# Dilated attention of a two-block transformer: tokens taken by residue modulo 4, 24 key tiles a head in place of 40

## The reference, cut to what matters

```python
ATTN_PATTERNS = ((128, 1), (512, 4), (2048, 16))      # (window, dilation); radius = window // (2 * dilation) = 64
...
# query at position p attends to p + j*dilation for j in [-radius, radius]
for g, (window, dilation) in enumerate(ATTN_PATTERNS):
    o_g, lse_g = dilated_window_attention(q[:, :, sl], k[:, :, sl], v[:, :, sl], dilation, window // (2 * dilation))
...
w_mix = jax.nn.softmax(jnp.stack(lses, axis=0), axis=0)
y_b = jnp.sum(w_mix[..., None] * o_all, axis=0)
```

## Time and profile before

| | |
|---|---|
| time of the runs | median 2284.1 us of three (2280.25 to 2287.16) |
| span of the profiled execution | 2278.1 us |
| what lies around the span | 6.0 us to the median, 2.2 to 9.1 us to the single runs |
| PE busy in the span | 2131.4 us (94%) |
| PEld busy | 1818.3 us (80%) |
| DVE, ACT busy | 963.5 us (42%), 830.5 us (36%) |
| attention stage | from 89.3 us to 430.2 us of the span |

### The profile page before, as it was taken

How to read it: one execution, slowest core, us unless ns; L and a number is a source line. 1 busy time by engine, 2 the same in 40 slices (tenths; PEclk the granted TensorE clock), 3 DMA queues, 4 the chain that set the end, 5 groups by cost and what they waited for, 6 DMA issues and landing times. The chain is left out here.

```text
span 2278.1 us, 27535 instructions
## 1 busy us (share of the span) xinstructions
PE 2131.4 (94%) x11313; PEld 1818.3 (80%) x11313; DVE 963.5 (42%) x1315; ACT 830.5 (36%) x1132; POOL 0.2 (0%) x4
## 2 busy tenths in 40 slices
PE   6899999999799999878888899999999978999999
PEld 5688888788788888777677888888779878888887
DVE  3544543233544434445653434434433334344343
ACT  4222332322432333336564343333344443423332
POOL 0000000000000000000000000000000000000000
PEclk9999999999899999988898999999999989999999
DMA  5222212123133222211011222332222212223222
GB/s 183 66 78 63 65 49 72 56 93 102 57 100 105 97 92 92 67 39 42 20 38 38 74 93 93 106 96 92 78 71 75 75 38 75 92 93 109 92 92 76
DMA packets 168319, 178.51 MB, mean 78 GB/s; under 512 B 5921, under 2 KB 138606, under 8 KB 168114
## 3 DMA queue, kind: packets, MB, share of 16 engines
q1 hardware_dynamic: 168088, 177.36, 24.6%
q10 hardware_dynamic: 154, 0.04, 0.0%
HBM read 175.29 MB, written 2.10 MB: 78 GB/s over the span
## 5 line engine op out<-in xcount | busy, mean ns | idle before, releaser
L83 PE MATMUL psum<-norm_T_hi,weights_hi 128*128 128x512 f32 x1184 | 469.1, 396 | 13.9 <-PEq L435 6.4
L85 PE MATMUL psum<-norm_T_hi,weights_lo 128*128 128x512 f32 x1184 | 462.0, 390 | 0.0
L84 PE MATMUL psum<-norm_T_lo,weights_hi 128*128 128x512 f32 x1184 | 461.8, 390 | 0.0
L83 PE MATMUL psum<-weights_hi,act_T_hi 128*128 128x512 f32 (+2 forms) x976 | 369.1, 378 | 8.4 <-DVE weights_lo L286 4.1
L84 PE MATMUL psum<-weights_lo,act_T_hi 128*128 128x512 f32 (+2 forms) x976 | 367.4, 376 | 0.0
L85 PE MATMUL psum<-weights_hi,act_T_lo 128*128 128x512 f32 (+2 forms) x976 | 367.2, 376 | 0.0
L1014 ACT ACTIVATE weights_hi<-raw_weights 128x2048 fp32r<-128x2048 f32 x96 | 183.5, 1911 | 359.7 <-PE psum L85 359.7
L83 PE MATMUL psum<-weights_hi,norm_T_hi 128*128 128x256 f32 (+2 forms) x928 | 267.9, 289 | 9.1 <-PEq L784 4.1
L83 PEld LDWEIGHTS psum<-norm_T_hi,weights_hi 128*128 128x128 f32 x1184 | 223.0, 188 | 64.8 <-issue 14.5
L1035 DVE TENSOR_TENSOR weights_lo<-raw_weights,weights_hi 128x2048 fp32r<-128x2048 f32 x96 | 220.1, 2293 | 111.3 <-ACT weights_hi L1014 111.1
L84 PE MATMUL psum<-weights_lo,norm_T_hi 128*128 128x256 f32 (+2 forms) x928 | 262.8, 283 | 0.0
(11 more groups left out here) (229 smaller groups left out, 1990.3 us busy)
## 6 DMA issues: line engine op xcount, KB each, us to landing
raw_weights<-in_ffn_w_dram SPq DMA_DIRECT2D x64, 1024.0 KB, 5.2
raw_weights<-in_w_in_dram SPq DMA_DIRECT2D x36, 512.0 KB, 4.5
raw_weights<-in_w_up_dram SPq DMA_DIRECT2D x16, 1024.0 KB, 5.4
raw_weights<-in_w_down_dram SPq DMA_DIRECT2D x16, 1024.0 KB, 5.1
raw_weights<-in_w_in_dram SPq DMA_DIRECT2D x12, 1024.0 KB, 5.1
raw_weights<-in_mlstm_w_in_dram SPq DMA_DIRECT2D x8, 1024.0 KB, 5.2
raw_weights<-in_w_out_dram SPq DMA_DIRECT2D x4, 1024.0 KB, 5.8
raw_weights<-in_mla_w_o_dram SPq DMA_DIRECT2D x4, 1024.0 KB, 5.3
```

Source lines behind the costliest of these rows:

```text
L83: pe.matmul(out, ah, bh, start=start, stop=False)
L84: pe.matmul(out, ah, bl, start=False, stop=False)
L85: return pe.matmul(out, al, bh, start=False, stop=stop)
```

## The change

Every tile of 128 tokens in this stage now holds the tokens of one residue modulo 4 (tokens t, t+4, t+8, ...) and no longer 128 neighbours.

- For groups 1 and 2 (dilation 4 and 16) only the key tile of the query's own residue is needed; group 0 (dilation 1) now needs all four. `key_tiles` gives 4 + 1 + 1 = 6 tiles for each query tile, 24 a head.
- Scores are three matmuls of 512, 128 and 128 columns into bank 2 and the first half of bank 3. The mask step is two operations, not three, and the maximum over the parts is folded into the scaling. `turn` and `values` take 6 tiles; ACT copies one bank and DVE half a bank.
- Fills 0 to 5 still multiply contiguous tokens. ACT writes their result to SBUF with a stride, so that queries and keys lie by residue.
- Fills 6 to 8 take their stationary operand with a stride: `tt` is every fourth token of `NTH` and `NTL`, 16 bytes apart.
- `store` reads PSUM with a stride on ACT and on DVE to put the tokens back in order. Mask and rotary tables are laid out anew; the mask table shrinks from 3 x 896 to 1152 columns.

```diff
 def key_tiles(g, t):
-    r = (RADIUS * DIL[g] + P - 1) // P
-    return max(0, t - r), min(NT, t + r + 1)
+    return (0, NT) if g == 0 else (t, t + 1)
...
                         for q, t in enumerate((2 * (f - 6), 2 * (f - 6) + 1) if f < 8 else range(NT)):
-                            tt = slice(t * P, t * P + P)
+                            tt = slice(t, S, NT)
...
-                        for g in range(NG):
+                        for g, at_bank in enumerate((PS[:, 2, :], PS[:, 3, 0:P], PS[:, 3, P:2 * P])):
                             lo, hi = key_tiles(g, t)
-                            mm = pe.matmul(PS[:, 2 + g, 0:(hi - lo) * P], QK[:, h % 2, g, 0, t * P:t * P + P],
+                            mm = pe.matmul(at_bank, QK[:, h % 2, g, 0, t * P:t * P + P],
...
-                            act.activation(QK[:, h % 2, f // 2, f % 2, :], bank, ACT.Copy).then_inc(ev.sem, 1)
+                            act.activation(QK[:, h % 2, f // 2, f % 2, :].rearrange("p (r i) -> p i r", r=NT),
+                                           bank.rearrange("p (i r) -> p i r", r=NT), ACT.Copy).then_inc(ev.sem, 1)
...
-                        act.activation(AH[:, 4 + h, :], PS[:, 6, :], ACT.Copy).then_inc(th.sem, 1)
+                        act.activation(AH[:, 4 + h, :], PS[:, 6, :].rearrange("p (r i) -> p i r", r=NT), ACT.Copy).then_inc(th.sem, 1)
...
-                            for b in (0, 2):
-                                act.wait_ge(ptr.sem, ptr.at(3 * i + b + 1))
-                                w = min(512, m - 512 * b)
-                                act.activation(PT[:, 512 * b:512 * b + w], PS[:, 2 + b, 0:w], ACT.Copy).then_inc(pte.sem, 1)
+                            act.wait_ge(ptr.sem, ptr.at(2 * i + 1))
+                            act.activation(PT[:, 0:512], PS[:, 2, :], ACT.Copy).then_inc(pte.sem, 1)
...
-                        dve.tensor_tensor(AL[:, 4 + h, :], PS[:, 6, :], AH[:, 4 + h, :].bitcast(F32), SUB).then_inc(tl.sem, 1)
+                        dve.tensor_tensor(AL[:, 4 + h, :], PS[:, 6, :].rearrange("p (r i) -> p i r", r=NT),
+                                          AH[:, 4 + h, :].bitcast(F32).rearrange("p (i r) -> p i r", r=NT), SUB).then_inc(tl.sem, 1)
...
-                            dve.tensor_reduce(mall, mx, AX.X, MAXOP).then_inc(a1.sem, 1)
-                            dve.wait_ge(a1.sem, a1.at(i + 1))
-                            dve.tensor_scalar(nm, mall, -scale, None, MUL).then_inc(smx.sem, 1)
+                            dve.wait_ge(smk.sem, smk.at(2 * (i + 1)))
+                            dve.tensor_scalar(nm, mx[:, 0:1], mx[:, 1:2], -scale, MAXOP, MUL).then_inc(smx.sem, 1)
...
-                            dve.tensor_copy(PT[:, 512:1024], PS[:, 3, :]).then_inc(bcd.sem, 1)
+                            dve.tensor_copy(PT[:, 512:768], PS[:, 3, 0:2 * P]).then_inc(bcd.sem, 1)
```

More of the change, by code:

```diff
@@ L34 @@
 NEG = -1e30
-MW = 896
+MW = 1152
 DIL = (1, 4, 16)
@@ L201, in build @@
         IDENT = sb("ident", [P, P])
-        MASK = sb("masks", [P, NG, MW], BF16)
+        MASK = sb("masks", [P, MW], BF16)
         CM = sb("chunk_masks", [P, 2, S])
@@ L205, in build @@
         SCR = sb("scratch", [P, 16384])
-        MRAW = SCR[:, 10240:10240 + NG * MW]
+        MRAW = SCR[:, 10240:10240 + MW]
         SM = sb("small", [P, 512])
@@ L505, in _ @@
                     dve.wait_ge(c_cast.sem, c_cast.at(32))
-                    dve.tensor_copy(MASK[:, :, :], MRAW.rearrange("p (g w) -> p g w", g=NG)).then_inc(smk.sem, 1)
+                    dve.tensor_copy(MASK[:, :], MRAW).then_inc(smk.sem, 1)
                     dve.wait_ge(rt.sem, rt.at(1))
@@ L544, in dilated @@
             VN = SCR[:, 6144:9216].rearrange("p (b t e) -> p b t e", b=2, t=NT)
-            SB = SCR[:, 9216:10624]
-            PT = SCR[:, 10624:12032]
+            NK = 6
+            SB = SCR[:, 9216:9216 + NK * P]
+            PT = SCR[:, 10624:10624 + NK * P]
             ON = SCR[:, 12032:12544].rearrange("p (t e) -> p t e", t=NT)
@@ L549, in dilated @@
             R1 = SCR[0:32, 13568:14592].rearrange("p (j s) -> p j s", j=2)
-            mx, mall = SM[:, 32:35], SM[:, 36:37]
+            mx = SM[:, 32:34]
             nm = SM[:, 38:39]
@@ L603, in scores @@
                         if i:
-                            pe.wait_ge(pte.sem, pte.at(2 * i))
+                            pe.wait_ge(pte.sem, pte.at(i))
                             pe.wait_ge(bcd.sem, bcd.at(i))
-                        for g in range(NG):
+                        for g, at_bank in enumerate((PS[:, 2, :], PS[:, 3, 0:P], PS[:, 3, P:2 * P])):
                             lo, hi = key_tiles(g, t)
-                            mm = pe.matmul(PS[:, 2 + g, 0:(hi - lo) * P], QK[:, h % 2, g, 0, t * P:t * P + P],
+                            mm = pe.matmul(at_bank, QK[:, h % 2, g, 0, t * P:t * P + P],
                                            QK[:, h % 2, g, 1, lo * P:hi * P], start=True, stop=True)
@@ L624, in values @@
                             pe.wait_ge(ev.sem, ev.at(NFILL * (h + 1)))
-                        pe.wait_ge(pte.sem, pte.at(2 * i + 2))
+                        pe.wait_ge(pte.sem, pte.at(i + 1))
                         pe.wait_ge(bcd.sem, bcd.at(i + 1))
@@ L744, in _ @@
                             dve.wait_ge(sc.sem, sc.at(i + 1))
[L745 to L753, removed]
-                            dve.tensor_reduce(mall, mx, AX.X, MAXOP).then_inc(a1.sem, 1)
-                            dve.wait_ge(a1.sem, a1.at(i + 1))
-                            dve.tensor_scalar(nm, mall, -scale, None, MUL).then_inc(smx.sem, 1)
+                            for c, (b, o, w, m0) in enumerate(((2, 0, 512, (NT - 1 - t) * P), (3, 512, 2 * P, 7 * P))):
+                                dve.tensor_tensor_reduce(SB[:, o:o + w], PS[:, b, 0:w], MASK[:, m0:m0 + w],
+                                                         1.0, -3.0e38, ADD, MAXOP, mx[:, c:c + 1]).then_inc(smk.sem, 1)
+                            dve.wait_ge(smk.sem, smk.at(2 * (i + 1)))
+                            dve.tensor_scalar(nm, mx[:, 0:1], mx[:, 1:2], -scale, MAXOP, MUL).then_inc(smx.sem, 1)
                             if more:
@@ L760, in _ @@
                                 store(h - 1)
-                            dve.wait_ge(ptr.sem, ptr.at(3 * i + 2))
-                            dve.tensor_copy(PT[:, 512:1024], PS[:, 3, :]).then_inc(bcd.sem, 1)
+                            dve.wait_ge(ptr.sem, ptr.at(2 * i + 2))
+                            dve.tensor_copy(PT[:, 512:768], PS[:, 3, 0:2 * P]).then_inc(bcd.sem, 1)
                             dve.reciprocal(rden, den).then_inc(rcp.sem, 1)
@@ L773, in _ @@
                     store(NH - 1)
-            stage_ld.passed(32); ev.passed(NFILL * NH + NT); tl.passed(NH); th.passed(NH); smk.passed(NG * NT * NH)
-            sc.passed(16); ond.passed(16); otd.passed(NH); ropes.passed(12); pex.passed(16); pte.passed(32)
-            ptr.passed(48); pvd.passed(16); smx.passed(16); v1.passed(36); a1.passed(16); rcp.passed(16)
+            stage_ld.passed(32); ev.passed(NFILL * NH + NT); tl.passed(NH); th.passed(NH); smk.passed(2 * NT * NH)
+            sc.passed(16); ond.passed(16); otd.passed(NH); ropes.passed(12); pex.passed(16); pte.passed(16)
+            ptr.passed(32); pvd.passed(16); smx.passed(16); v1.passed(36); rcp.passed(16)
             bcd.passed(16)
@@ L1901, in constants @@
     i = np.arange(P)[:, None]
[L1902 to L1908, removed]
+    j = np.arange(P)[None, :]
+    ok = [np.abs(NT * (j - i) + d) <= RADIUS for d in range(1 - NT, NT)]
+    ok.append(np.abs(j - i) * NT <= RADIUS * DIL[1])
+    ok.append((NT * (j - i) % DIL[2] == 0) & (np.abs(j - i) * NT <= RADIUS * DIL[2]))
+    c["c_masks"] = np.where(np.concatenate(ok, 1), 0.0, NEG).astype(np.float32)
     j = np.arange(S)[None, :] - (S - P)
@@ L1921, in constants @@
     a = angles(16, 500000.0, 32)
+    a = a.reshape(P, NT, 16).transpose(1, 0, 2).reshape(S, 16)
     cs, sn = np.cos(a).astype(np.float32), np.sin(a).astype(np.float32)
```

## The result

| | before | changed |
|---|---|---|
| median of the runs | 2284.61 us (4 runs, 2280.25 to 2287.16) | 2351.25 us (4 runs, 2349.41 to 2352.09) |
| ratio of the runs | 1 | 1.0296, 95% interval 1.0281 to 1.0311 |
| span of the profiled execution | 2278.1 us | 2348.7 us |
| attention stage, first matmul to the next stage's | 340.95 us (89.29 to 430.24, rows 10 and 9) | 405.72 us (88.91 to 494.63) |

The loss is 66.6 us between the medians; in the profiled executions the attention stage is 64.8 us longer. The sign and the mechanism were forecast, the size was not: 2330 us was predicted, and the time lies 9 us above the range.

A forecast was written before the change was run, and what follows sets the result against it. TensorE's stream was taken to bound the attention stage. Savings of 34.3 us, 0.5 us for the last `store` and 81.8 us for strided loads gave +48.0 us, 2284.1 to 2332, stated as 2330 us; range 2245 to 2342.

The forecast's parts named there:

- What bounds the stage: Attention stage: as long as TensorE's stream, busy 331.7 of 337 us; fills 0 to 5 bound by moving columns, fill 8 by weight loads.
- The savings: TensorE's path in the attention stage: scores 12.9 us, transposes 7.0 us and values 14.4 us less, together 34.3 us.
- cover ahead of the transposes: Mask step to first transpose: the fill in between covers TensorE's possible wait, with 1.9 us to spare.
- ACT's and DVE's strides at nothing: ACT's strided query and key copies cost nothing, 14 us without cover; the last `store`, read with a stride, adds 0.5 us.
- The strided load: Fills 6 to 8: 768 loads with every fourth token take 0.222 us between neighbours, adding 81.8 us.
- The upper bound of 0.228 us: Fills 6 to 8: a load crossing all 512 columns at the moving stream's rate takes 0.228 us, adding 86.4 us.
- The ratio of 1.65: VectorE's 1.73 over 1.05 ns, if it held for TensorE: loads 0.18 us apart, a loss of some 15 us.
- The clock: Rival: loads cost more than double or fill 8 lowers the granted clock, adding 10 to 20 us, 2340 to 2350; chance 0.06.
- The free stride: Rival for the loads of fills 6 to 8: the stride costs nothing, only savings count, 2250 us; chance 0.36.
- the part cost: Rival: loads stretched to 1.3 to 1.5 times cost 27 to 35 us against 34, 2276 to 2286 us; chance 0.08.
- the savings that do not come through: Rival: TensorE waits for the mask chain or weight splits; needs ACT copies over 5 us each; no chance of its own.
- The low end of the forecast: Fills 6 to 8: loads stretched to 1.6 to 1.8 times, giving 2298 to 2315 us.

## Why the prediction was right in sign and wrong in size

- **What bounds the stage: right.** TensorE's stream before and after. The waits of its matmuls for the copies that the profile names are these two, 3.0 us in all of the changed kernel's stage (total us, times, longest), and the kernel before has the same two with 3.1 us:

```profile
PE psum L630 <- ACT scratch L701: 1.7, 3, 0.6
...
PE psum L630 <- DVE scratch L755: 1.3, 1, 1.3
```

- **The savings: right as prices, but not all of them came through.** At full clock scores are 1.31 us a tile (the earlier trace rows gave 1.98 and 2.36), so 4 x (2 x 0.67 + 2 x 1.05) = 13.8 us where I took 12.9; values 1.33 us a tile as foreseen. With 7.0 us for the transposes and 14.4 for the values that makes 35.2 us. Against it stand the late starts of `values`, 2.1 us in the changed kernel and 3.5 us in the one with plain tokens. So 2250.25 us measured against 2250 is in part luck: two errors cancel, and the stage of that run is 31.3 us shorter, not 33.8. The prediction had looked for cover ahead of the transposes alone; the pauses came one step later, ahead of `values`.
- **ACT's and DVE's strides at nothing: nearly right.** L674 did nearly double (1092 ns), and its cover left 1.4 us. The last `store` took no more than before (1.64 us, 492.99 to 494.63), where I had put 0.5 us.
- **The strided load: the step that failed.** The prediction took "a load at half its rate, 0.222 us between neighbours, near the upper end". It measured 0.2335 us, so the term is 384 x 0.1225 + 384 x 0.1135 = 90.6 us and not 81.8. The upper bound of 0.228 us was itself wrong, and so was its reason: I let the load cross 512 columns at the rate of the moving stream. The run with every eighth value shows that the span hardly counts, and the one with a strided moving operand that the two ports have different prices, so a row of the one was no bound for the other. The ratio of 1.65 that I had worked out from the Trainium skill, "Vector Engine (DVE) Microarchitecture Reference", under "The SBUF access granule: adjacent pairs", did not carry over either: here it is 2.10 for loads and 2.02 for the moving operand.
- **The clock: named and not added, the second step that failed.** I put it in a rival of 0.06 with 10 to 20 us, though I had tied it there to loads of 0.22 us in fill 8, which were the forecast's own. It goes with the slow load in fill 8, and cost 7.6 us.
- **The sum with these terms:** -35.2 + 2.1 + 90.6 + 7.6 = 65.1 us, where the stage of the profiles is 64.8 us longer. The forecast had 48.0. Of the 17 us between them half is the load's price and most of the other half the clock.
- **The rivals.** The free stride did not happen, nor the part cost; of the savings that do not come through, about a tenth did at most, as above. The low end of the forecast was added up wrongly: at the prediction's prices a stretch to 1.6 to 1.8 gives 2284.1 - 33.8 + 768 x 0.1155 x (0.6 to 0.8), some 2303 to 2321 us and not 2298 to 2315. That changes nothing in the outcome.

The 1.8 us between the stage's 64.8 and the 66.6 of the medians were not traced. In the two profiled executions the stages behind the attention, whose instructions are the same, differ by 6.2 us (2348.7 - 494.63 against 2278.1 - 430.24), which is more than the medians leave for them.

## What to carry to other kernels

Where loads of a stationary operand set the pace (here 128 and 256 moving columns for each), lay the operand out so that its values are neighbours; count the 16-byte lines it touches, at 1.82 ns a line here, once that is more than the 0.87 ns of each value. Put a change of order where there is slack and where it is cheap: on ACT's or DVE's read from PSUM it cost at most 22 ns a copy. Cover is to be looked for at every place: three of the 24 strided writes held up TensorE, through two steps of another engine. And before a product keeps its small moving width only because of the layout that its result needs, price the other way round plus a transpose: with 512 moving columns and 48 transposes the values became cheaper than with plain stationary tokens, as the kernel before makes them.

## What the runs showed of the hardware that was not expected

- A lone 4-byte value in its line costs 1.82 ns on TensorE's stationary side and 0.90 ns on its moving side.
- ACT copied 512 values in 599 ns with a step of 16 bytes on the PSUM read, and in 1092 ns with the hops on the SBUF write.
- With loads at 0.2335 us the granted clock held at 1.00 with 256 columns for each and fell to 0.50 with 128. It was still low for the first scores behind, which took 2.66 us and not 1.31.
- With a step of 12 bytes the load's distance was 0.178 us at full clock and 0.215 us at half clock; with a step of 16 bytes it did not change. Why is open; it was not tried further.
